# A three-layer fp32 block on one core: a chunk of adaLN work, the gelus and an output projection moved

## What is computed

```python
# layer 1
proj = rms_norm(x) @ w_in                    # q, k, v, pool, gm_u, gm_v, 3 gates
merged = g0*(o_sb @ w_br_sb) + g1*(o_pool @ w_br_pool) + g2*(o_gm @ w_br_gm)
#   o_gm = gelu(u) * (W_s @ norm(gelu(v)) + b);  g = sigmoid(gate_in)
x = x + rms_norm(merged @ w_out)
x = x + rms_norm(square(relu(rms_norm(x) @ w_ff_in)) @ w_ff_out)
# layers 2 and 3, i = 0 and 1
mod = silu(c) @ ada_w[i] + ada_b[i]          # 6 vectors: sh1, sc1, g1, sh2, sc2, g2
x = x + g1 * mixer(rms_norm(x) * (1+sc1) + sh1)     # i=0: conformer conv; i=1: attention, 16 heads
x = x + g2 * (square(relu(h @ mlp_w1[i])) @ mlp_w2[i])
```

## Time and profile before

| | |
|---|---|
| profiled execution | 1104.98 us |
| its span in the trace | 1103.2 us |
| PE busy | 1053.0 us, 95% |
| DVE busy | 702.4 us, 64% |
| ACT busy | 492.0 us, 45% |
| granted TensorE clock, mean | 0.982 |
| moved from HBM | 215.07 MB, 196 GB/s over the span |
| chain that ended last | PE 83%, DVE 7%, ACT 5%, issue 2%, DMA 2% |

### The profile page before, as it was taken

The page is one execution under the profiler, slowest core; times in us unless marked ns, Lnnn a source line. Parts: engine busy times, 40 slices in busy tenths (PEclk is TensorE's granted clock), DMA queues, the critical chain, the costliest instruction groups (busy, mean ns, idle before and its releaser), DMA issues.

```text
span 1103.2 us, 16804 instructions
## 1 busy us (share of the span) xinstructions
PE 1053.0 (95%) x6872; PEld 930.4 (84%) x6872; DVE 702.4 (64%) x829; ACT 492.0 (45%) x554; POOL 110.7 (10%) x78
## 2 busy tenths in 40 slices
PE   6999998999999999997899999999998799999998
PEld 6997776899999989975789999998786479999996
DVE  5758556687667677653478765776674748454463
ACT  6355536444344445330454344435444834444441
POOL 0030002010010030025001001000000401100000
PEclk9999999999999999998899999999999899999999
DMA  8884335738787772878128787782553324556540
GB/s 301 293 302 149 118 116 171 271 120 317 257 289 271 269 233 84 233 211 278 65 74 330 280 288 256 281 295 86 191 191 116 114 77 148 196 171 198 188 166 39
DMA packets 118204, 221.58 MB, mean 201 GB/s; under 512 B 6338, under 2 KB 20740, under 8 KB 118148
## 3 DMA queue, kind: packets, MB, share of 16 engines
q1 hardware_dynamic: 115888, 212.88, 56.7%
q0 software_dynamic: 2064, 7.86, 2.2%
q10 hardware_dynamic: 196, 0.05, 0.0%
HBM read 215.07 MB, written 1.05 MB: 196 GB/s over the span
## 4 chain that ended last, share of the span: by engine, by line
PE 83%; DVE 7%; ACT 5%; issue 2%; DMA 2%; ACTq 0%; DVEq 0%
PE ps L410 78%; ACT hi L348 2%; PE ps L865 2%; DMA ada_raw<-in_ada_w 2%; PE ps L447 1%; PE ps L724 1%; DVE lo L359 1%; DVE mid_acc L888 1%; DVE ada_acc L888 1%; DVE stat L1911 1%; PE ps L650 0%; DVE hTl L497 0%; ACT aS L1607 0%; DVE aS L1906 0%; ACT gate L1508 0%
## 5 line engine op out<-in xcount | busy, mean ns | idle before, releaser
L359 DVE TENSOR_TENSOR lo<-raw,hi 128x2048 fp32r<-128x2048 f32 x153 | 357.5, 2343 | 285.0 <-ACT hi L348 284.2
L348 ACT ACTIVATE hi<-raw 128x2048 fp32r<-128x2048 f32 x153 | 292.4, 1913 | 336.7 <-PE ps L410 318.7
L410 PE MATMUL ps<-hTh,hi 128*128 128x256 f32 x992 | 282.7, 285 | 2.0 <-DVE hTl L497 1.9
L410 PE MATMUL ps<-hTh,lo 128*128 128x256 f32 x992 | 280.7, 283 | 0.0
L410 PE MATMUL ps<-hTl,hi 128*128 128x256 f32 x992 | 280.7, 283 | 0.0
L410 PEld LDWEIGHTS ps<-hTh,hi 128*128 128x128 f32 x992 | 190.2, 192 | 3.8 <-DVE hTl L497 2.5
L410 PEld LDWEIGHTS ps<-hTl,hi 128*128 128x128 f32 x992 | 190.3, 192 | 0.3
L410 PEld LDWEIGHTS ps<-hTh,lo 128*128 128x128 f32 x992 | 190.3, 192 | 0.0
L410 PE MATMUL ps<-hi,hidh 128*128 128x512 f32 x416 | 162.8, 391 | 0.4 <-DVEq L645 0.4
L410 PE MATMUL ps<-hi,hidl 128*128 128x512 f32 x416 | 162.1, 390 | 0.0
L410 PE MATMUL ps<-lo,hidh 128*128 128x512 f32 x416 | 162.0, 389 | 0.0
(11 more groups left out here) (219 smaller groups left out, 889.8 us busy)
## 6 DMA issues: line engine op xcount, KB each, us to landing
raw<-in_mlp_w SPq DMA_DIRECT2D x64, 1024.0 KB, 5.3
ada_raw<-in_ada_w SPq DMA_DIRECT2D x42, 1024.0 KB, 7.3
raw<-in_w_in SPq DMA_DIRECT2D x21, 1024.0 KB, 7.3
raw<-in_w_ff_in SPq DMA_DIRECT2D x16, 1024.0 KB, 5.3
raw<-in_w_ff_out SPq DMA_DIRECT2D x16, 1024.0 KB, 6.8
raw<-in_attn_w_qkv SPq DMA_DIRECT2D x12, 1024.0 KB, 5.7
raw<-in_conv_w_in SPq DMA_DIRECT2D x8, 1024.0 KB, 5.4
ada_raw<-in_ada_w POOLq DMA_DIRECT2D x6, 1024.0 KB, 8.2
```

What stands on the lines that cost most here:

```text
L348: nc.scalar.activation(hi[:, slot], raw[:, slot], ACT.Copy).then_inc(hi_made, 1)
L359: nc.vector.tensor_tensor(lo[:, slot], raw[:, slot], hi[:, slot].bitcast(F32), ALU.subtract).then_inc(lo_made, 1)
L410: return nc.tensor.matmul(o, lhs, rhs, start=start, stop=False, skip_group_check=True)
```

## The change

1. The gelus are one activation each on ACT (`Gelu_apprx_tanh`), with a table load ahead of the two; DVE's six operations and ACT's four go. PE waits for `gelu_done` in place of `gelu_dve`.
2. Chunk 10 is now layer 0's column block 10 and is done in the first MLP's last units, chunk 21 (column block 9 of layer 1) in the second MLP's (`ADA_LAST`). `ADA_MID` has two chunks (11, 12) in place of three, `ADA_QKV` is gone. The conv's `mid_acc[2]`, its loads, `mid_unit(dve, 2, ...)` and its `ada_sum` are gone, and POOL makes the stationaries 4 to 7 without loads between them. POOL's start on `dw_sel` waits for chunk 10 in place of 9.
3. The attention's output projection has its units by rows (the four columns k=0..3 first), with `out_unit(0, 0)` inside round 9 and `out_unit(0, 1)` inside round 10, the other two behind the rounds. It writes banks 4 to 7; `stay_warm` of that norm uses bank 0; the order of the loads follows.

```diff
+        GELUS = "gelu_apprx_tanh_and_others"
@@ mlp_pe
-            second(1, n + 4, n + 4, 8 * m + 8, final=True)
+            def last_sum():
+                if m:
+                    pe.wait_ge(row_kept, 2)
+                ada_sum(pe, ADA_LAST[m][0])
+
+            second(1, n + 4, n + 4, 8 * m + 8, (last_sum if m < 2 else None, None), final=True)
@@
-        ADA_MID = [(10 + q, 1, 6 + q) for q in range(3)]
-        ADA_QKV = (21, 1, 9)
-        ADA_HEAD = ((2, 0, 8), (13, 0, 10), (22, 1, 10))
-        ADA_TAIL = ((9, 0, 9), (20, 0, 11), (23, 1, 11))
+        ADA_MID = [(11, 0, 11), (12, 1, 6)]
+        ADA_HEAD = ((2, 0, 8), (13, 1, 7), (22, 1, 10))
+        ADA_TAIL = ((9, 0, 9), (20, 1, 8), (23, 1, 11))
+        ADA_LAST = ((10, 0, 10), (21, 1, 9))
@@ mlp_dve
+                if j == 3:
+                    ada_unit(dve, ADA_LAST[m][0], 1, skip(m))
                 dve_step(dve, u0 + 26 + j)
                 if j == 1:
                     lo_of(1, 8 * m + 7)
                 if j == 2:
                     ada_keep(dve, ADA_TAIL[m])
+                    if m < 2:
+                        ada_unit(dve, ADA_LAST[m][0], 0, skip(m))
+            if m < 2:
+                ada_keep(dve, ADA_LAST[m])
@@ sync, conv input projection (and the same behind the qkv loads of c == 1, with ADA_LAST[1])
                     cin(c, h)
+                    if c == 1:
+                        ada_load(sp, ADA_LAST[0], h)
@@ tensor, conv stage
-            ada_sum(pe, ADA_MID[2][0], mid_acc[2], 0)
@@ tensor, qkv
             def first_unit_done():
-                ada_sum(pe, ADA_QKV[0])
-                pe.wait_ge(ada_kept, ADA_QKV[0] + 2)
                 gate_row(pe, 1, 0)
@@ tensor, rounds
+            def out_unit(h, c):
+                unit_x(pe, U_WO + 2 * h + c, None, hTh, hTl, 4 * h,
+                       lambda tt, _: y_bank(tt, c, 4), h == 0, final=c == 1 and h == 1,
+                       need=56 if c == 0 else None)
...
+                if s == PAIRS + 1:
+                    pe.wait_ge(s_arg, AT_HEADS)
+                    out_unit(0, 0)
+                if s == PAIRS + 2:
+                    out_unit(0, 1)
+            out_unit(1, 0)
+            out_unit(1, 1)
-            square(U_WO, 7, True)
@@ scalar
-            def gelu_parts(i, x):
-                nc.scalar.activation(gt[:, 0], x, ACT.Square).then_inc(gelu_act, 1)
-                act.wait_ge(gelu_dve, 2 * i + 1)
-                nc.scalar.activation(gt[:, 1], gt[:, 0], ACT.Sigmoid, scale=GELU_2C).then_inc(gelu_act, 1)
+            def gelu(x, dst):
+                nc.scalar.activation(dst, x, ACT.Gelu_apprx_tanh).then_inc(gelu_done, 1)
+            nc.scalar.preload_act_table_set(GELUS)
@@ vector, conv stage
-                if k in (1, 3):
-                    mid_unit(dve, 2, k // 2)
-            ada_keep(dve, ADA_MID[2], 0)
@@ gpsimd, conv stage
-            mid_load(pool, 2, 0)
-            stationaries(4)
-            stationaries(5)
-            mid_load(pool, 2, 1)
-            stationaries(6)
-            stationaries(7)
+            for k in range(4, KT):
+                stationaries(k)
```

More of the change, by code:

```diff
@@ L31 @@
 RSQRT_MAGIC = 1597463007.0
-GELU_2C = 2.0 * float(np.sqrt(2.0 / np.pi))
-GELU_A = 0.044715
 HD = 64
@@ L198, in build_kernel @@
         dw_sel = ada_area("dw_sel", 8192, [P, 2, TAP_GROUPS, STRIPS, CH])
-        mid_acc = [hid_area("mid_acc0", 8192, [P, 512]), ada_acc, row_area("mid_acc2", 6144, [P, 512])]
+        mid_acc = [hid_area("mid_acc0", 8192, [P, 512]), ada_acc]
         Qs = big("Qs", 0, [P, TT, D])
@@ L281, in build_kernel @@
         p_kept = sem("p_kept")
-        gelu_act = sem("gelu_act")
-        gelu_dve = sem("gelu_dve")
+        gelu_done = sem("gelu_done")
         gate_kept = sem("gate_kept")
@@ L654, in norm_pe, with y_bank @@
                 pe.wait_ge(row_kept, 2)
-            stay_warm((16, 34, 36, 14, 14, 14)[norm])
+            stay_warm((16, 34, 36, 14, 14, 14)[norm], bank=0 if norm == 5 else 7)
             transposes(pe, lambda tt, k: X[:, tt, k * P:(k + 1) * P],
                        [(diag_ok, norm + 1)] * 2, diag_n)
-        def y_bank(tt, c):
-            return ps[:, 2 * tt + c]
+        def y_bank(tt, c, base=0):
+            return ps[:, base + 2 * tt + c]
         def y_half(tt, c):
@@ L702, in post_dve, with gated_dve @@
                                                    op1=ALU.add).then_inc(x_ver, 1)
-        def gated_dve(dve, which, last, row, norm=True):
+        def gated_dve(dve, which, last, row, norm=True, base=0):
             for tt, c in QUARTERS:
@@ L708, in gated_dve @@
                 y, x = y_half(tt, c), halves(X, tt)[c]
-                link(dve, nc.vector.tensor_tensor(y, y_bank(tt, c), row[:, 512 * c:512 * c + 512], ALU.mult))
+                link(dve, nc.vector.tensor_tensor(y, y_bank(tt, c, base), row[:, 512 * c:512 * c + 512], ALU.mult))
                 ins = nc.vector.tensor_tensor(x, x, y, ALU.add)
@@ L720, in gate_row @@
         def gate_row(pe, layer, i):
-            pe.wait_ge(ada_kept, (10, 21, 22, 24)[2 * layer + i] + 1)
+            pe.wait_ge(ada_kept, (11, 21, 22, 24)[2 * layer + i] + 1)
             for k in range(KT):
@@ L1122, in _ @@
                          rows3(attn_w_qkv_2[0])[:, 4 * h:4 * h + 4, 512 * c:512 * c + 512])
-                    if c == 0:
-                        ada_load(sp, ADA_QKV, h)
-            square(U_WO, attn_w_o_2[0])
+                    if c == 1:
+                        ada_load(sp, ADA_LAST[1], h)
+            for h in range(2):
+                for c in range(2):
+                    load(sp, U_WO + 2 * h + c, rows3(attn_w_o_2[0])[:, 4 * h:4 * h + 4, 512 * c:512 * c + 512])
             mlp_sp(sp, 2, mlp_w1_2[1], mlp_w2_2[1], (s_z, AT_HEADS))
@@ L1208, in _ @@
                     pe.wait_ge(p_kept, 1)
-                    pe.wait_ge(gelu_dve, 2)
+                    pe.wait_ge(gelu_done, 1)
                 elif s == 2:
-                    pe.wait_ge(gelu_dve, 4)
+                    pe.wait_ge(gelu_done, 2)
                 elif s % 2 == 0:
@@ L1457, in _ @@
                                  ACT.Copy).then_inc(p_kept, 1)
-            gelu_parts(0, ps[:, 1])
+            gelu(ps[:, 1], gu[:].rearrange("p k n -> p (k n)"))
             act_step(act, 8)
-            act.wait_ge(gelu_dve, 2)
-            gelu_parts(1, ps[:, 2])
+            gelu(ps[:, 2], gv[:].rearrange("p t n -> p (t n)"))
             nc.scalar.preload_act_table_set("natural_log_exp_and_others")
@@ L1467, in softplus @@
                 if h < 2:
-                    act.wait_ge(gelu_dve, 4)
+                    act.wait_ge(gelu_done, 2)
                 else:
@@ L1657, in _ @@
             ada_keep(dve, ADA_IN[1])
-            def gelu(i, x, dst):
-                dve.wait_ge(gelu_act, 2 * i + 1)
-                link(dve, nc.vector.tensor_scalar(gt[:, 0], gt[:, 0], GELU_A, 1.0, ALU.mult, ALU.add))
-                nc.vector.tensor_tensor(gt[:, 0], gt[:, 0], x, ALU.mult).then_inc(gelu_dve, 1)
-                dve.wait_ge(gelu_act, 2 * i + 2)
-                nc.vector.tensor_tensor(dst, gt[:, 1], x, ALU.mult).then_inc(gelu_dve, 1)
-            gelu(0, ps[:, 1], gu[:].rearrange("p k n -> p (k n)"))
             dve_step(dve, 8)
-            gelu(1, ps[:, 2], gv[:].rearrange("p t n -> p (t n)"))
             def gating_norm():
-                dve.wait_ge(gelu_dve, 4)
+                dve.wait_ge(gelu_done, 2)
                 dve.wait_ge(misc_in, 16 * N_MISC_DMAS)
@@ L1873, in _ @@
             for c in range(6):
-                if c == 1:
-                    ada_keep(dve, ADA_QKV)
                 for h in range(2):
                     dve_step(dve, U_QKV + 2 * c + h)
-                    if c == 0:
-                        ada_unit(dve, ADA_QKV[0], h, skip(1))
                 if c < 4:
@@ L1929, in _ @@
             dve.wait_ge(row_kept, 3)
-            gated_dve(dve, 4, U_WO + 3, row_a)
+            gated_dve(dve, 4, U_WO + 3, row_a, base=4)
             mod_hT(6, 8, 1, 3, U_WO + 3, ADA_HEAD[2])
```

## The result

The changed kernel takes 1095.42 us (median of five runs, 1094.64 to 1096.18), the kernel before, timed beside it, 1103.76 (1100.35 to 1104.84). The ratio is 0.9933 with a 95% interval of [0.9914, 0.9951]: faster, by 7.4 us where 13.75 were forecast. Against the predicted 1090.0 us it is 5.4 us slow, just inside the upper end of the range; the ratio times 1103.76 gives 1096.4, just outside it.

The account below looks back on a forecast made before the run. PE, busy 95% of the span, was taken as the bound; -1.15 + 1.65 - 8.7 + 0.85 - 5.0 - 1.4 = -13.75 took the profiled 1104.98 to 1091.2, or 1090.0 us from the median, range 1086.0 to 1096.0.

Parts of the forecast that it names:

- A: Gelu stage: one activation per gelu removes PE's 1.17 us stop before suffix(0); -1.15 us, bounds -1.2 and +0.5.
- B: End of first MLP: the added chunk's sum on PE and POOL's products beside DVE cost +1.65 us, bounds +0.85 and +4.0.
- C: Conv stage: PE does the last moments right behind conv(3) at full clock instead of waiting; -8.7 us, bounds -9.5 and -5.
- 1.7 in full, twice: Conv stage's -5 bound: the up to 1.7 us by which POOL's product may lengthen DVE's half, counted fully two times.
- D: End of second MLP: one more ada_sum on PE, +0.85 us, bounds +0.8 and +2.
- E: qkv: without chunk 21 gate_row follows unit 107 at once and the next unit runs faster; -5.0 us, bounds -5.1 and -4.
- F: Attention's last rounds: two output projection units moved into the rounds let the residual end earlier; -1.4 us, bounds -2.2 and +2.
- Rival 1: Conv stage gives back less because taps or dw_sel become the wait; C -5, B at upper part, 1095 us, chance 0.17.
- Rival 2: Clock stays up in the conv's output projection, some 2 us come back; 1088 us, chance 0.12.
- Rival 3: F fails: the norm behind the rounds starts at half clock, +2 in place of -1.4; 1093.4 us, chance 0.10.
- Rival 4: Slower than before: new chunks' half 1 lands late, PE stands between both MLPs' last two units; 1109.3 us, chance 0.03.
- Rival 5: Chunk and gelu stops are only replaced, e.g. the gate row still waits for chunk 21; about 1102 us, chance 0.05.

Follow-up runs that it names:

- e3: Changed kernel with POOL's first two dw_sel products held until after norm 2's transposes, not beside the first MLP's residual; one run 1096.9 us.
- c1: e2 plus stay_warm(30) ahead of the conv's output projection and POOL's first two dw_sel products behind norm 2's last hTl; 1086.88 us, ratio 0.9837.
- e1: Changed kernel with POOL starting stationaries(4) only when DVE has done the last half of chunk 12; one run 1091.49 us.
- e2: Changed kernel with PE doing conv(2) ahead of the second mid chunk's sum and moments(0); 1085.6 us, ratio 0.9841.
- third execution: Changed kernel profiled a third time, nothing edited; 1092.8 us in a single execution, conv stage 55.40 us.
- p10: Kernel before with only chunk 10 moved to the first MLP's end and two chunks in the conv stage; 1101.06 us over eleven runs, ratio 0.9969.
- a3: Changed kernel with the attention's output projection back behind the rounds and by columns; 1096.26 us, ratio 0.9928.
- e4: Changed kernel with stay_warm(30) in place of stay_warm(18) ahead of the conv's output projection; one run 1091.18 us.
- a1: Changed kernel with the gelus as before, ACT and DVE in turns; 1095.26 us, ratio 0.9923.
- a2: Changed kernel with chunk 21 back under the qkv projection, the second MLP's end without it; 1095.82 us, ratio 0.9935.
- a4: Changed kernel with three chunks in the conv stage again and none in the first MLP's last units; 1097.39 us, ratio 0.9933.
- p21: Kernel before with only chunk 21 moved to the second MLP's end; 1098.51 us, ratio 0.9949.

## Why the prediction was right and wrong

The forecast of the profiled execution was 1091.2 us and it took 1095.8. Of these 4.6 us the conv stage is 3.06, and the two stretches of layer 1 without any part of the change are 2.56; the others gave back 1.05. The remaining 0.8 us to the median come from the median of before, which stood 1.2 under its profile where the changed kernel's stands 0.4 under.

**A** was right: the stop is gone and nothing replaced it. The gain of about 1.5 us (143.8 to 143.9 in both executions before, 142.2 to 142.5 in three after) is larger than the stop of 1.17, which was taken as the limit. Of the 1.51 us, 1.25 lie where the stop was (between the second and the third pair of groups of `ps<-qT,kT` matmuls) and 0.24 in the 30 us behind the first adaLN sum, whose length differs as much between the changed kernel's own executions (30.25 to 30.50). The gelu's price, for which only a Sigmoid's row of 0.63 stood, was 0.57 to 0.59.

**B** was right in size, +1.41 for +1.65, and in its parts: 0.8 us of it was POOL beside DVE (e3 and c1 take just that away), the rest the sum on PE. The operation hit was the scaling one alone. The Trainium skill (SBUF — State Buffer, "SBUF: two separate sides") says that whichever starts first gets the shared port pair for its whole instruction and the other waits. The trace agrees: the split began at 413.39, POOL's product at 413.57, and POOL was the loser, with 5.76 us for two products; only the scaling, begun behind the split, waited. The +2.8 that the prediction worked out from the lock took both DVE operations for losers, and that did not come.

**C** is the step that failed. The mechanism forecast for the gain was right: moments(2) and (3) directly behind conv(3), at full clock, in 3.56 us (521.86 to 525.42) where 3.9 were said. The failed term is the +0.5 for POOL's products beside DVE's half: "may lengthen it by up to 1.7, which PE's ada_sum of that chunk sees; ... I take +0.5 for both". The case was named and a price known from rows, for one product, and then a third of it was taken. What came: DVE's half was lengthened by 3.24 us (6.35 - 3.11), because its four short operations in a row met two products, not one (`stationaries(5)` no longer waits for a load either); PE stood 3.46 us in place of 0.22, and the clock, forecast at 1.00 throughout, was 0.50 for 3.4 us behind the stop. e1 shows the cause (POOL held back: stop 0.22, half 3.11), e2 that only PE's order made it a cost. e2 also gives the size: with no idle and no low clock the stage takes 48.72 us, so the stop and its clock cost 5.46 us (54.18 - 48.72) where 0.5 was taken. That the stage missed its forecast of 51.1 us (59.8 - 8.7) by 3.06 only is luck: without the 0.5 the forecast stands at 50.6, 1.9 above e2, among other things since the waits of 0.22, 0.18 and 0.59 us ahead of the second sum, conv(2) and conv(3) went too. With the lengthening that the prediction calls "1.7 in full, twice", its own sum gives 515.5 + 3.4 + 3.9 = 522.8, or -5.8 (the bound is written as -5, and the one of no cost as -9.5, where the same sum gives -9.2); measured was -5.64. In the third execution, and in p10, it was -4.4 and -4.0, with 6.8 us at clock 0.50 behind the stop.

**D** and **E** were right: +0.97 for +0.85, -5.14 for -5.0. E's stretch is 60.83 to 60.88 in all thirteen profiles that have the edit, D's 198.65 to 198.69 in twelve of them (198.95 in a3).

**F** was right: -1.07 for -1.4, with the norm's idle at 1.54 for 1.6 and no slow pace behind it.

**Rivals.** Rival 1's number (1095, with C at -5) is what came, and its ground, POOL's products beside DVE, was the cause; but PE waited for DVE's chunk and not for dw_sel, and B was not at its upper part. Rival 2, the clock of the conv's projection, came in by 0.8 of 2 us; the idle of 2.9 stayed, and e4 shows that taking it away gives 0.3 to 1.0 more. Rivals 3, 4 and 5 did not come: the new halves landed in time.

**What the sum left out** is the scatter. One execution was subtracted from one execution, and code with no part in the change differed by 2.56 us between the two. Within one program the first adaLN sum comes at 47.12 to 48.73 us. The totals show the same: in the last round three executions of the kernel before took 1100.1 to 1100.8 us at a mean granted clock of 0.989, four took 1104.5 to 1106.8 at 0.982 to 0.984, and both its profiles are of 0.982. All twelve of the changed kernel are at 0.987 or 0.989. So the -9.2 of the profiles is measured from the longer kind; from the shorter kind the gain is some 5 us, and the medians of before (1103.3 to 1105.0) lie between or at the longer. What stays open is why the totals of a1, a2 and a4 lie nearer to the changed kernel than their stretches say. Their intervals are some 2 us to either side, which covers a1, not quite a2 and a4. That stops cost more or less clock with the place at which the low clock falls is shown, and a2's profile has 20.5 us at clock 0.50 against the changed kernel's 23.9; that this sums to the missing 2 to 4 us is not.

## What to carry to other kernels

When an edit removes a wait from one engine's queue, list what that queue does earlier and which short operations of its neighbour now run beside it: a chain of four short DVE operations in front of a PE instruction can pay for two POOL instructions in full. If the price of a collision is known from rows, take it in full, once for each instruction that can fall across the chain, unless something excludes it. The cheap repair is often to give the waiting engine other ready work first (conv(2) ahead of the sum, 5.5 to 6.7 us) rather than to slow the neighbour, and where PE must stand for 2.9 us or more, filler matmuls saved the clock of what follows (0.3 to 1.0 us at the conv's projection, up to 2.3 at layer 1's). Before subtracting one profile from another, compare the granted clock of the same stretch in both.

## What the runs showed of the hardware

- DVE operations with both operands in SBUF wait for a POOL product that is under way: the half 6.35 us for 3.11, two cacc 2.47 for 0.76, one of 128x8 1.81 for 0.16. One that reads PSUM does not: in e2, two cacc from PSUM at 505.00 took 0.86 us with a POOL product from 504.01 to 505.92, and 0.87 in the changed kernel at 502.57 without one. Both ways it holds: POOL's two products took 5.76 us behind a split and 4.06 in e1, where DVE waited for them.

```profile
504.01 1.91 POOL L1982 TENSOR_TENSOR dw_sel<-cst,pcol 128x1024 f32<-128x1024 f32 x1 [1.54 <-PE ps L407]
...
505.00 0.86 DVE L1836 SCALAR_TENSOR_TENSOR cacc<-ps,pcol,cmean 128x256 f32<-128x256 f32 x2
```

- A stop of PE of 3.46 or 3.6 us comes with a granted clock of 0.50 for 3.4 or 6.8 us, begun in the stop or up to 2.0 us behind its end, in every profile. It costs about half of the part in which PE has matmuls ready, from nothing to 2.3 us in executions of one program. After 2.90 us the projection lost 0.3 to 1.0 us to it, and the stop of 1.92 us in qkv was followed by 3.4 us at 0.50 in all four profiles that have it. Shorter stops are not safe in every execution: those of 0.92 and 0.93 us in the last rounds of the kernel before brought no low clock in its two profiles, but 0.50 from 880.6 to 884.0 in p21's. After the 1.54 us ahead of norm 5 in the changed kernel the clock stayed at 1.00.
- At the start PE's first 128x128 matmuls follow each other at 0.21 us and later ones at 0.11, though the granted clock of the rows reads 1.00. The moment of the change differs between executions: in the changed kernel's three the first norm's transposes start at 14.2 to 15.8 us, and the first adaLN sum 32.9 us behind them.
- An activation table load takes 1.28 us and the next activation follows at once: in the changed kernel one starts at 69.67, 0.03 us behind the end of the activation before it, and the next ACT operation starts at 70.96. The second runs from 76.23 to 77.51.
